# A delta-rule and attention kernel: the activation table is asked for ahead of each logarithm and exponential of the norms, not once per loop

## The chip, the cores and the metric

The kernel runs on one core of a Trainium2 chip. The metric is the device time of one execution in microseconds (us). The engines of the core have their own instruction streams and meet at semaphores: TensorE (PE, with its weight loads as PEld), VectorE (DVE), ScalarE (ACT), GpSimd (POOL) and SyncE (SP), which issues most of the DMAs. ScalarE evaluates functions such as exp, ln and tanh from a table set that is loaded into the engine by an instruction of its own, `ACT_TABLE_LOAD`.

## What is computed

512 tokens of width 1024 go through two blocks of the first kind (retention, forgetting attention, RWKV-7, a gated feed-forward part) and one of the second kind. The change touches only the second kind. Its mixer, cut to what matters:

```python
qkv_a, qkv_b, z_b, beta_b, alpha_b, gate_a, gate_b = split_columns(h @ w_in, IN_WIDTHS)
qa = rms_norm(qkv_a[:, :, 0], q_norm)            # local (dilated window) attention, 3 groups
ka = rms_norm(qkv_a[:, :, 1], k_norm)
...
qkv_b = causal_short_conv(qkv_b, conv_w)         # 4 taps, then SiLU
qb = l2_norm(qb.reshape(b, s, 8, 128)) * (128 ** -0.5)
kb = l2_norm(kb.reshape(b, s, 8, 128))
o_b = gated_delta_rule(qb, kb, vb, beta, g)      # chunked, 64 tokens each
o_b = rms_norm(o_b, dn_out_norm) * jax.nn.silu(z_b.reshape(b, s, 8, 128))
```

Each norm multiplies x by rsqrt(mean or sum of x*x, plus 1e-6) and a gain.

## The kernel before

Activations are kept transposed: 128 channels on the partitions, 512 tokens along the free axis, one tile of 128x512 per chunk of channels. The large projections are a stream ("flow") of units. A unit is one output tile: 8 columns of 128x128 weights, each multiplied three times (head by head, head by rest, rest by head, lines 370 to 372), since float32 weights and activations are split into a head and a rest. The weights of a piece (512 KB) are loaded by SP into one of four raw slots, ACT copies the head (`flow_head`, line 389) and DVE subtracts it for the rest (`flow_rest`, line 400).

All other stages are written into the same instruction streams. `flow.pe(t)`, `flow.act(t)` and `flow.dve(t)` put out everything of the flow that is due before tick t on their engine, at the place where they are called. What a unit leaves to ACT and DVE (evictions, convolution taps, the tanh of a gate) is a list of functions with due times, and it is put out in the same way. So the order on every engine is fixed when the program is built, and each engine works strictly in that order.

`unit_norm` (line 1921) is the norm of the window attention, of q and k of the delta rule, and of its output. It loops over n chunks (8 for q and k, 4 for the output). ACT squares a chunk (`square`, line 1950), PE sums the squares over the partitions (line 1935), ACT takes the logarithm out of the PSUM bank (line 1961) and then exp(-0.5 log) (`root`, line 1943), and DVE multiplies (line 1972). Squares are put out two chunks ahead of the logarithm. The names are `dn_sq`, `dn_rs` for q and k, `out_sq`, `out_rs` for the output and `win_sq`, `win_rs` for the windows. Between two chunks stands `flow.act`, with which the flow may put out a tanh there, of the convolution (`squash`, line 1826), or of the gates (line 1853).

`k.tables(name)` puts out a table load only where the set asked for is another than the one asked for last:

```python
def __call__(self, name):
    if name != self.held:
        self.nc.scalar.preload_act_table_set(name)
        self.held = name
```

`LN_EXP` names a set with ln and exp, `EXP_TANH` one with exp and tanh. Loads of this helper have line 420. Where a function stands in the program that the set at that place does not hold, a load is put ahead of it when the program is built, and it has the line of the function. The delta rule runs in two halves of four heads. In each, `unit_norm` for q and k is followed by `delta_pairs` (line 2368), whose PE part begins as follows and whose exponentials are `er` (line 2469) and `dl` (line 2471):

```python
pe.wait_ge(*k.gates_ready.at(2))
pe.wait_ge(*k.signals["un_log"].at(8))
```

Then follow the inversion of the triangular blocks, with four legs of small DMAs from ACT's queue (`blocks`, `spare_lanes`, `blocks_back`, `low_t`), the scan, and `unit_norm` for the output.

Of the kernel before, what the change touches and what calls it, by code (L numbers as in the profile page):

```python
# [41 lines left out]
LN_EXP = "natural_log_exp_and_others"  # L42
# [128 lines left out]
class Mark:  # L171
# [19 lines left out]
    def at(self, n):  # L191
        return self.sem, self.base + n
# [1728 lines left out]
def unit_norm(k, chunks, sums, scale, done, at, after=None):  # L1921


    nc, ps, flow, pe, v, a = k.nc, k.ps, k.flow, k.pe, k.v, k.a
    squared, summed, log, rstd = k.marks("un_squared", "un_sums", "un_log", "un_rstd")
    sq, rs, n = k.norm_sq, k.norm_rs, len(chunks)
    slots, roots = sq.shape[1], rs.shape[1]

    def tensor_part():
        for j in range(n):  # L1930
            flow.pe(at(j / n))
            pe.wait_ge(*squared.at(j + 1))
            if j >= 4:
                pe.wait_ge(*log.at(j - 3))
            nc.tensor.matmul(ps[j % 4][:, :], sums, sq[:, j % slots, :], start=True, stop=True).then_inc(*summed.up())  # L1935
        flow.pe(at(1))

    def scalar_part():
        k.tables(LN_EXP)

        def root(j):
            a.wait_ge(*log.at(j + 1))
            nc.scalar.activation(rs[:, j % roots, :], rs[:, j % roots, :], ACT.Exp, scale=-0.5).then_inc(*rstd.up())

        def square(j):
            if j >= slots:
                a.wait_ge(*summed.at(j - slots + 1))
            if chunks[j][3]:
                a.wait_ge(*chunks[j][3])
            nc.scalar.activation(sq[:, j % slots, :], chunks[j][0], ACT.Square).then_inc(*squared.up())  # L1950

        if after:
            a.wait_ge(*after)
        square(0)
        square(1)
        for j in range(n):
            flow.act(at(j / n))
            a.wait_ge(*summed.at(j + 1))
            if j >= roots:
                a.wait_ge(*done.at(done_base + j - roots + 1))  # L1960
            nc.scalar.activation(rs[:, j % roots, :], ps[j % 4][:, :], ACT.Ln, bias=k.const["eps6"], scale=scale).then_inc(*log.up())
            if j + 2 < n:
                square(j + 2)
            root(j)
        flow.act(at(1))

    def vector_part():
        for j in range(n):
            flow.dve(at((j + .5) / n))
            v.wait_ge(*rstd.at(j + 1))  # L1970
            src, gain, dst, _ = chunks[j]
            nc.vector.scalar_tensor_tensor(dst, src, gain, rs[:, j % roots, :], ALU.mult, ALU.mult).then_inc(*done.up())
        flow.dve(at(1))

    done_base = done.total - done.base
    tensor_part()
    scalar_part()
    vector_part()

# [1596 lines left out]
```

## Time and profile before

| | us |
|---|---|
| median of 3 runs | 3169.86 |
| lowest and highest of them | 3167.87, 3171.47 |
| span of the profiled execution | 3170.7 |
| PE busy in it | 2900.4 (91%) |
| DVE busy | 1704.2 (54%) |
| ACT busy | 1252.6 (40%) |
| table loads on ACT | 55 |

The span is the time from the first to the last instruction of one profiled execution. Starts are in us from its beginning. Busy shares are averages over stages with quite different limits, so the stages of the delta rule (about 2265 to 2630 us) are read one by one. The granted clock of TensorE is a share of full speed: 1.00 is 2.4 GHz and 0.50 is 1.2 GHz.

### The profile page before, as it was taken

The page shows a single profiled execution, that of the slowest core. Times are in us where ns is not written, and L with a number is a line of the kernel's source. Part 1 is how long each engine was busy: PE and PEld are TensorE (multiplying, and loading weights), DVE is VectorE, ACT ScalarE, POOL GpSimd, SP SyncE. Part 2 cuts the span into 40 slices and gives each one's busy share as a digit, 9 for nine tenths or more (in the row PEclk, how much of TensorE's full clock was granted, in tenths as well). Part 3 has the DMA queues.
Part 4 walks back from the last instruction along what each step waited for, and adds up shares of the span by engine and source line. Part 5 has one row for each costly group of instructions (what it writes and reads, how often), then busy time and mean ns, then how long its engine had stood idle before and what let it go on. Part 6 is the DMA issues. An engine that isn't in the chain of part 4 may idle for free.

```text
span 3170.7 us, 35407 instructions
## 1 busy us (share of the span) xinstructions
PE 2900.4 (91%) x13998; PEld 2291.2 (72%) x13998; DVE 1704.2 (54%) x2469; ACT 1252.6 (40%) x1913; POOL 14.8 (0%) x22
## 2 busy tenths in 40 slices
PE   6998899999999987999999999997688799969997
PEld 5566677888886666778888877775477677858885
DVE  3456535555334565355554335456574545459995
ACT  3233233333221342334332224454534434348873
POOL 0000000000000000000000000000000000000000
PEclk9999899999999999999999999998889899989998
DMA  4112113233331112022233321111110112359981
GB/s 162 47 40 63 44 41 93 97 96 100 92 124 62 44 51 63 28 89 88 98 99 114 99 94 54 60 60 47 33 47 28 45 36 87 98 216 370 396 323 53
DMA packets 96180, 307.70 MB, mean 97 GB/s; under 512 B 25744, under 2 KB 31760, under 8 KB 84240
## 3 DMA queue, kind: packets, MB, share of 16 engines
q1 hardware_dynamic: 69056, 284.88, 26.7%
q10 hardware_dynamic: 24368, 11.12, 1.2%
q0 software_dynamic: 2592, 9.44, 0.8%
q8 instruction: 112, 1.84, 0.2%
q14 instruction: 52, 0.43, 0.0%
HBM read 296.49 MB, written 8.91 MB: 96 GB/s over the span
## 4 chain that ended last, share of the span: by engine, by line
PE 77%; DVE 10%; ACT 6%; issue 4%; DMA 1%; ACTq 1%; POOL 0%; POOLq 0%; DVEq 0%
PE bank L370 19%; PE bank L372 18%; PE bank L371 18%; PE bank L365 2%; PE bank L367 2%; PE bank L366 2%; ACT flow_head L389 2%; DVE flow_rest L400 2%; PE bank L1935 1%; DVE dn L1818 1%; PE bank L2532 1%; PE bank L1238 1%; PE bank L1072 1%; PE bank L559 1%; PE bank L2017 0%
## 5 line engine op out<-in xcount | busy, mean ns | idle before, releaser
L400 DVE TENSOR_TENSOR flow_rest<-flow_raw,flow_head 128x1024 fp32r<-128x1024 f32 (+2 forms) x372 | 438.5, 1179 | 940.1 <-ACT flow_head L389 940.0
L370 PE MATMUL bank<-h_head,flow_head 128*128 128x512 f32 x2144 | 898.8, 419 | 34.2 <-DVE flow_rest L400 24.7
L371 PE MATMUL bank<-h_rest,flow_head 128*128 128x512 f32 x2144 | 846.7, 395 | 0.0
L372 PE MATMUL bank<-h_head,flow_rest 128*128 128x512 f32 x2144 | 846.3, 395 | 0.0
L389 ACT ACTIVATE flow_head<-flow_raw 128x1024 fp32r<-128x1024 f32 (+2 forms) x372 | 379.2, 1019 | 724.4 <-PE bank L372 677.2
L370 PEld LDWEIGHTS bank<-h_head,flow_head 128*128 128x128 f32 x2144 | 410.9, 192 | 155.1 <-issue 61.4
L371 PEld LDWEIGHTS bank<-h_rest,flow_head 128*128 128x128 f32 x2144 | 410.5, 191 | 92.0 <-issue 16.5
L372 PEld LDWEIGHTS bank<-h_head,flow_rest 128*128 128x128 f32 x2144 | 408.7, 191 | 89.0
L372 PE MATMUL bank<-ff_head,flow_rest 128*128 128x512 f32 x352 | 137.1, 389 | 0.0
L370 PE MATMUL bank<-ff_head,flow_head 128*128 128x512 f32 x352 | 137.1, 389 | 0.0
L371 PE MATMUL bank<-ff_rest,flow_head 128*128 128x512 f32 x352 | 137.1, 389 | 0.0
L400 DVE TENSOR_TENSOR flow_rest<-ring,flow_head 128x1024 fp32r<-128x1024 f32 x90 | 107.6, 1221 | 20.8 <-ACT flow_head L389 17.9
L400 DVE TENSOR_TENSOR late_rest<-ring,late_head 128x1024 fp32r<-128x1024 f32 x88 | 105.0, 1219 | 2.1 <-ACT late_head L389 0.4
L389 ACT ACTIVATE flow_head<-ring 128x1024 fp32r<-128x1024 f32 x90 | 94.7, 1061 | 22.0 <-PE bank L367 19.8
L389 ACT ACTIVATE late_head<-ring 128x1024 fp32r<-128x1024 f32 x88 | 93.3, 1062 | 18.9 <-PE bank L367 14.1
L370 PE MATMUL bank<-mh,flow_head 128*128 128x512 f32 x192 | 77.8, 405 | 5.9 <-DVE mr L1597 5.4
L1664 ACT ACTIVATE ff_head<-ff_up 128x512 fp32r<-128x512 f32 x44 | 27.8, 633 | 138.1 <-DVE ff_up L1660 138.1
L370 PE MATMUL bank<-yh,flow_head 128*128 128x512 f32 x96 | 43.8, 456 | 36.2 <-DVE sgf L1566 36.2
L371 PE MATMUL bank<-mr,flow_head 128*128 128x512 f32 x192 | 76.5, 398 | 0.0
L372 PE MATMUL bank<-mh,flow_rest 128*128 128x512 f32 x192 | 76.4, 398 | 0.0
L371 PEld LDWEIGHTS bank<-ff_rest,flow_head 128*128 128x128 f32 x352 | 66.1, 188 | 13.8
L372 PEld LDWEIGHTS bank<-ff_head,flow_rest 128*128 128x128 f32 x352 | 66.1, 188 | 13.7
(607 smaller groups left out, 4206.0 us busy)
## 6 DMA issues: line engine op xcount, KB each, us to landing
flow_raw<-in_w_in SPq DMA_DIRECT2D x176, 512.0 KB, 3.4
ring<-in_experts SPq DMA_DIRECT2D x84, 1024.0 KB, 7.3
flow_raw<-in_w_gate_up SPq DMA_DIRECT2D x88, 512.0 KB, 3.4
flow_raw<-in_w_down SPq DMA_DIRECT2D x32, 512.0 KB, 3.5
flow_raw<-in_w_out SPq DMA_DIRECT2D x24, 512.0 KB, 3.5
flow_raw<-in_paths SPq DMA_DIRECT2D x24, 256.0 KB, 2.6
flow_raw<-in_w_down SPq DMA_DIRECT2D x16, 384.0 KB, 3.1
flow_raw<-in_path_b SPq DMA_DIRECT2D x8, 512.0 KB, 3.4
```

The source lines that it names most:

```text
L365: nc.tensor.matmul(ps[bank][:, :], head, wh[:, c:c + S], start=start, stop=False)
L366: nc.tensor.matmul(ps[bank][:, :], head, wr[:, c:c + S], start=False, stop=False)
L367: last = nc.tensor.matmul(ps[bank][:, :], rest, wh[:, c:c + S], start=False, stop=stop)
L370: nc.tensor.matmul(ps[u.bank][:, :], wh[:, c:c + P], head, start=start, stop=False)
L371: nc.tensor.matmul(ps[u.bank][:, :], wh[:, c:c + P], rest, start=False, stop=False)
L372: last = nc.tensor.matmul(ps[u.bank][:, :], wr[:, c:c + P], head, start=False, stop=stop)
L389: nc.scalar.activation(self.parts_of[p.slot][0][:, 0:p.words], p.raw, ACT.Copy).then_inc(self.heads, 1)
L400: nc.vector.tensor_tensor(self.parts_of[p.slot][1][:, 0:p.words], p.raw, f32(self.parts_of[p.slot][0][:, 0:p.words]), ALU.subtract).then_i ...
L559: nc.tensor.matmul(ps[h // 2][b:b + HD, kt * P:S], v_tok[:, kt, h * HD:(h + 1) * HD], weighted[:, u % 4, 0:S - kt * P], start=kt == 0, sto ...
L1072: last = nc.tensor.matmul(ps[u % 4][:, q * 256:(q + 1) * 256], m[b:b + HD, jn, :], ar[b:b + HD, jn, :, :], start=True, stop=True)
L1238: last = nc.tensor.matmul(BX[c][:, m * P:m * P + n], CT[c][:, m, :], T[c][:, m, 0:n], start=True, stop=True)
L1818: ins = nc.vector.scalar_tensor_tensor(dst, k.pad[:, b, j:j + S], tap[:, j:j + 1], dst, ALU.mult, ALU.add)
```

## The change

`unit_norm` asks for the set `LN_EXP` in two more places: at the head of `root`, ahead of the exponential, and in the loop behind `flow.act`, ahead of the wait for the sum and the logarithm.

```diff
@@ -1939,6 +1939,7 @@
         k.tables(LN_EXP)
 
         def root(j):
+            k.tables(LN_EXP)
             a.wait_ge(*log.at(j + 1))
             nc.scalar.activation(rs[:, j % roots, :], rs[:, j % roots, :], ACT.Exp, scale=-0.5).then_inc(*rstd.up())
 
@@ -1955,6 +1956,7 @@
         square(1)
         for j in range(n):
             flow.act(at(j / n))
+            k.tables(LN_EXP)
             a.wait_ge(*summed.at(j + 1))
             if j >= roots:
                 a.wait_ge(*done.at(done_base + j - roots + 1))
```

Only ACT's stream differs; those of PE, DVE, SP and POOL hold the same instructions in the same order. ACT has 55 table loads before and 43 after, and every difference lies at three places.

ACT, norm of q and k of the first half, from the tanh of a convolution (line 1826) to the exponential of the fifth chunk; before:

```order
L1826 ACTIVATE sgf_179<-dn_0_185 128x512
L1961 ACT_TABLE_LOAD
L1961 ACTIVATE dn_rs<-bank,base_table 128x512
L1950 ACTIVATE dn_sq<-dn_1_183 128x512
L1943 ACT_TABLE_LOAD
L1943 ACTIVATE dn_rs<-dn_rs 128x512
L389 ACTIVATE flow_head<-flow_raw 128x1024
L1961 ACT_TABLE_LOAD
L1961 ACTIVATE dn_rs<-bank,base_table 128x512
L1950 ACTIVATE dn_sq<-dn_1_183 128x512
L1943 ACT_TABLE_LOAD
L1943 ACTIVATE dn_rs<-dn_rs 128x512
```

After, at the same place (logarithm, exponential and square now have lines 1963, 1944 and 1951):

```order
L1826 ACTIVATE sgf_179<-dn_0_185 128x512
L420 ACT_TABLE_LOAD
L1963 ACTIVATE dn_rs<-bank,base_table 128x512
L1951 ACTIVATE dn_sq<-dn_1_183 128x512
L1944 ACTIVATE dn_rs<-dn_rs 128x512
L389 ACTIVATE flow_head<-flow_raw 128x1024
L1963 ACTIVATE dn_rs<-bank,base_table 128x512
L1951 ACTIVATE dn_sq<-dn_1_183 128x512
L1944 ACTIVATE dn_rs<-dn_rs 128x512
```

One load stands behind the tanh where before each logarithm and each exponential up to the end of the loop had its own (ten in this norm).

ACT, end of the same norm and the first exponentials of `delta_pairs`; before:

```order
L1961 ACT_TABLE_LOAD
L1961 ACTIVATE dn_rs<-bank,base_table 128x512
L1943 ACT_TABLE_LOAD
L1943 ACTIVATE dn_rs<-dn_rs 128x512
L1826 ACTIVATE sgf_179<-dn_0_185 128x512
L2469 ACTIVATE er<-bank 128x512
```

After (`er` is line 2471 now):

```order
L1963 ACTIVATE dn_rs<-bank,base_table 128x512
L1944 ACTIVATE dn_rs<-dn_rs 128x512
L420 ACT_TABLE_LOAD
L1826 ACTIVATE sgf_179<-dn_0_185 128x512
L2471 ACTIVATE er<-bank 128x512
```

The tanh behind the loop has a load of its own now, since the set asked for last is `LN_EXP`.

ACT, norm of the first half's output and the beginning of the norm of q and k of the second half; before:

```order
L1826 ACTIVATE sgf_179<-dn_2_187 128x512
L1961 ACT_TABLE_LOAD
L1961 ACTIVATE out_rs<-bank,base_table 128x512
L1943 ACT_TABLE_LOAD
L1943 ACTIVATE out_rs<-out_rs 128x512
L389 ACTIVATE flow_head<-flow_raw 128x1024
L1961 ACT_TABLE_LOAD
L1961 ACTIVATE out_rs<-bank,base_table 128x512
L1943 ACT_TABLE_LOAD
L1943 ACTIVATE out_rs<-out_rs 128x512
L1853 ACTIVATE sgf_179<-sgf_179 128x512
L420 ACT_TABLE_LOAD
```

After:

```order
L1826 ACTIVATE sgf_179<-dn_2_187 128x512
L420 ACT_TABLE_LOAD
L1963 ACTIVATE out_rs<-bank,base_table 128x512
L1944 ACTIVATE out_rs<-out_rs 128x512
L389 ACTIVATE flow_head<-flow_raw 128x1024
L1963 ACTIVATE out_rs<-bank,base_table 128x512
L1944 ACTIVATE out_rs<-out_rs 128x512
L420 ACT_TABLE_LOAD
L1853 ACTIVATE sgf_179<-sgf_179 128x512
L420 ACT_TABLE_LOAD
```

Three loads are gone and one has come ahead of the tanh of line 1853. The third place, the last two chunks of the norm of q and k of the second half, has the same pattern: four loads of lines 1961 and 1943 become one, and one comes ahead of the next tanh of line 1853, behind three pairs of `er` and `dl`.

## Rows read from the trace of the kernel before

**Rows 1.** The page, part 1: busy time, share of the span, instructions.

```profile
PE 2900.4 (91%) x13998; PEld 2291.2 (72%) x13998; DVE 1704.2 (54%) x2469; ACT 1252.6 (40%) x1913; POOL 14.8 (0%) x22
```

**Rows 2.** Groups of ACT: count | busy us, mean ns | idle us before.

```profile
L420 ACT ACT_TABLE_LOAD x37 | 47.5, 1283 | 4.7 <-issue 4.1
...
L1961 ACT ACT_TABLE_LOAD x9 | 11.5, 1283 | 0.2
L1943 ACT ACT_TABLE_LOAD x9 | 11.5, 1283 | 0.2
```

**Rows 3.** Chain of waits, 2277.1 to 2300.1 us: shares of the stretch by line.

```profile
by line: ACT L1961 27.9%; issue 24.7%; ACT dn_rs L1961 15.0%; ACT L1943 11.5%; ACT dn_rs L1943 7.9%; ACT flow_head L389 4.5%; ACT dn L1813 3.1%; ACT sgf L1826 2.7%; ACT dn_sq L1950 2.7%; PE bank L2397 2.4%; ACT L420 2.0%; ACTq L1960 0.1%
```

**Rows 4.** Timeline of ACT, first half's norm: start, us, instruction, [idle before].

```profile
2280.96 0.62 ACT L1950 ACTIVATE dn_sq<-dn 128x512 f32<-128x512 f32 x1
2281.60 1.28 ACT L1943 ACT_TABLE_LOAD   x1
...
2282.89 0.63 ACT L1943 ACTIVATE dn_rs<-dn_rs 128x512 f32<-128x512 f32 x1
...
2283.43 1.04 ACT L389 ACTIVATE flow_head<-flow_raw 128x1024 fp32r<-128x1024 f32 x1
...
2293.37 0.63 ACT L1943 ACTIVATE dn_rs<-dn_rs 128x512 f32<-128x512 f32 x1
...
2295.32 0.69 ACT L1961 ACTIVATE dn_rs<-bank,base_table 128x512 f32<-128x512 f32 x1
...
2299.26 0.69 ACT L1961 ACTIVATE dn_rs<-bank,base_table 128x512 f32<-128x512 f32 x1
```

**Rows 5.** Timeline of ACT where no load stands between the functions.

```profile
2274.37 0.62 ACT L1950 ACTIVATE dn_sq<-dn 128x512 f32<-128x512 f32 x1
2274.89 0.62 ACT L1943 ACTIVATE dn_rs<-dn_rs 128x512 f32<-128x512 f32 x1
2275.41 0.68 ACT L1961 ACTIVATE dn_rs<-bank,base_table 128x512 f32<-128x512 f32 x1
...
2622.35 0.69 ACT L1961 ACTIVATE out_rs<-bank,base_table 128x512 f32<-128x512 f32 x1 [0.46 <-PE bank L1935]
2623.07 0.63 ACT L1943 ACTIVATE out_rs<-out_rs 128x512 f32<-128x512 f32 x1
```

**Rows 6.** Timeline of PE, first half's norm and the start of `delta_pairs`.

```profile
2287.04 2.08 PE L1935 MATMUL bank<-dn_sq,base_table 128*128 128x512 f32 x2 [3.58 <-ACT dn_sq L1950]
...
2292.11 1.13 PE L1935 MATMUL bank<-dn_sq,base_table 128*128 128x512 f32 x2 [1.09 <-ACT dn_sq L1950]
...
2300.09 2.05 PE L2397 MATMUL bank<-table_2b,g 128*128 128x128 f32 x8 [6.16 <-ACT dn_rs L1961]
```

**Rows 7.** Timeline of DVE, the same stretch.

```profile
2284.50 1.22 DVE L400 TENSOR_TENSOR flow_rest<-flow_raw,flow_head 128x1024 fp32r<-128x1024 f32 x1 [4.71 <-ACT flow_head L389]
2285.64 0.74 DVE L1972 SCALAR_TENSOR_TENSOR dn<-dn,base_table,dn_rs 128x512 f32<-128x512 f32 x1
...
2286.31 0.68 DVE L1809 TENSOR_TENSOR pad<-bank,root 128x512 f32<-128x512 f32 x1
...
2294.71 2.32 DVE L1818 SCALAR_TENSOR_TENSOR dn<-pad,pk,dn 128x512 f32<-128x512 f32 x3
...
2303.98 0.69 DVE L2440 TENSOR_TENSOR kb<-dn,bank 128x512 f32<-128x512 f32 x1 [1.31 <-PE bank L2403]
```

**Rows 8.** By stretch: us, busy of ACT, granted clock, DMA share, GB/s.

```profile
2300.09:2303.50 3.41, 2.79 (x4) 0.50 0.00 0
```

**Rows 9.** Timeline of PE: first sum and first `delta_pairs` product, second half.

```profile
2461.42 2.08 PE L1935 MATMUL bank<-dn_sq,base_table 128*128 128x512 f32 x2 [9.88 <-ACT dn_sq L1950]
...
2484.94 2.05 PE L2397 MATMUL bank<-table_2b,g 128*128 128x128 f32 x8 [5.68 <-ACT dn_rs L1961]
```

**Rows 10.** Timeline of PE: a sum of a window norm behind a shorter wait.

```profile
2105.78 2.08 PE L1935 MATMUL bank<-win_sq,table_2b 128*128 128x512 f32 x2 [2.67 <-ACT win_sq L1950]
```

**Rows 11.** DMA issues, 2330 to 2372 us: KB each, median us to landing.

```profile
flow_raw<-in_w_in SPq DMA_DIRECT2D x4, 512.0 KB, 3.5
blocks<-low_t ACTq DMA_DIRECT2D x8, 16.0 KB, 1.7
```

## The prediction

> **What bounds the kernel now.** I read the page first. PE is busy for 91% of the span and ACT for 40% [rows 1], which says only that ACT is no bound on the average. What counts is whether ACT is the bound where the loads stand. The groups of ACT show 55 table loads of 1.283 us each, 37 asked for by the kernel and 18 put ahead of a logarithm or an exponential of `unit_norm` (nine and nine) [rows 2]. The idle time ahead of these 18 is 0.2 us in each group, so ACT goes straight from the function before into the load.
>
> The chain of waits over 2277.1 to 2300.1 us is almost nothing but ACT: loads of lines 1961, 1943 and 420, then the functions they serve [rows 3]. PE waits there: 3.58 us, 1.09 us and then 6.16 us for ACT [rows 6]. The same picture stands in the second half: PE waits 9.88 us for the first square of the second norm and 5.68 us for its last logarithm [rows 9]. At all three places ACT sets the end, and DVE and PE behind it can only start later or earlier by what ACT does.
>
> **What the change does.** Only ACT's stream changes. Of the 18 loads all go; three come back behind the tanh inside the loops, and three come ahead of the tanh that follows each place. The net is 12 loads, 12 x 1.283 = 15.4 us of ACT's busy time.
>
> **Price of a load on the path.** From a square to the exponential behind it is 2282.89 - 2280.96 = 1.93 us with a load between [rows 4] and 2274.89 - 2274.37 = 0.52 us without [rows 5]. So a load costs 1.41 us: its own 1.28, and about 0.1 us by which two neighbours would have overlapped. From an exponential to a logarithm it is 2295.32 - 2293.37 = 1.95 us [rows 4] against 0.52 us [rows 5], a price of 1.43. From a logarithm to its own exponential there is no overlap to win (0.72 us without a load, 2623.07 - 2622.35 [rows 5]); there it is the load alone, 1.28.
>
> The Trainium skill, "ScalarE: Activation LUTs", section "What ACT_TABLE_LOAD costs", gives some 1.28 us for the load and 1.38 us for a drain, about 2.66 us for each switch. The load agrees with this trace; the drain does not, since the load here begins 0.02 us after the end of the square, at 2281.60, and the exponential begins 0.01 us after the load. By the page's total the three places would give about twice my sum, an estimate of some 30 us.
>
> **First place, norm of q and k, first half.** The load at 2279.08 stays under another line. Up to the last logarithm at 2299.26, which releases PE's first product of `delta_pairs` at 2300.09, eight loads go: seven at 1.41 to 1.43 and one, between a logarithm and its exponential, at 1.28. That is 11.1 us.
>
> Not all of it comes, as one cover is gone. The last tap of the convolution (line 1813, on ACT) needs `pad` from DVE, and before it came late enough. Now the exponential is at 2280.96 + 0.52 = 2281.48 and `flow_head` at 2282.0. DVE follows by the distances of [rows 4, 7]: `flow_rest` 1.07 us later (2283.07), the multiply 1.14 later (2284.21), `pad` 0.67 later (2284.88), done at 2285.6. ACT would be free for the tap at 2284.6 (logarithm 2283.0, square 2283.6, exponential 2284.1). It waits about 1.0 us. The last logarithm comes at about 2289.1 and PE starts `delta_pairs` 0.83 us behind it, as now (2300.09 - 2299.26), at 2289.9: 10.2 us earlier.
>
> There is a second part on PE. After its wait of 6.16 us the granted clock is 0.50, the lower level of 1.2 GHz, for the 3.41 us to 2303.5 [rows 6, 8], while it did not fall behind the wait of 1.09 us (two sums in 1.13 us against 2.08 us) [rows 6]. Squares now come early, so that by the same walk PE's waits in this norm are 0.9 us at most; I take the clock to stay at 2.4 GHz. Then the products of lines 2397 and 2403 take 1.9 us instead of 3.8 and end at 2291.8. The next step, `kb` on DVE, needs these and the last multiply. DVE, in its order, does the sixth multiply at 2288.0, the three taps (2.32 us [rows 7]), the seventh multiply at 2290.9 and the eighth at 2291.6, and so reaches `kb` at 2292.3, against 2303.98 [rows 7]: 11.7 us earlier. DVE's multiplies hide the rest of PE's gain. If the clock falls after all, it is 10.2.
>
> The load that comes ahead of the tanh of line 1826 has `er` queued behind it, and DVE's next step after `kb` waits for `er`. Last exponential 2289.8, load 2290.5 to 2291.8, tanh 2291.8, `er` 2292.3 to 2292.9, and DVE wants it at 2292.9. It is covered by the multiplies and by `kb`, without a margin; with that cover gone it costs up to 1.3 us. I take 0.1. First place: **11.6 us**, between 8.9 and 11.7.
>
> **Second place, norm of the output, first half.** Three loads go ahead of the tanh of line 1853 (1.28 between logarithm and exponential, 1.41 behind `flow_head`, 1.28 again) and one comes ahead of it (1.41 back). The next load, ahead of the squares of the second norm, stays. PE waits for just these squares. Net 4.0 - 1.4 = **2.5 us**, rounded down for small gaps. The tanh needs a DVE step that by the same distances is ready at the time the added load ends, so nothing new waits, and the wait of 9.88 us stays above 7: PE's clock is at 1.2 GHz behind it as before.
>
> **Third place, last two chunks of the second norm.** Two loads stand ahead of the last logarithm that PE waits for: 1.28 + 1.43 = **2.7 us**. The third is ahead of the last exponential, off the path. The added load comes ahead of a tanh in the middle of `delta_pairs`, where PE is full and ACT waits for DVE; I cost it at nothing, 0.2 us without that cover. PE's wait falls from 5.68 to 3.0 us [rows 9]. The row nearest to that is a wait of 2.67 us with the same 2.08 us for two sums behind it [rows 10], so the clock falls here still. If not, 1.7 us more.
>
> **Sum.** 11.6 + 2.5 + 2.7 = 16.8 us; the ends are 8.9 + 2.5 + 2.7 = 14.1 and 11.7 + 2.6 + 4.4 = 18.7. What follows is carried by semaphores from these points, and the chain of waits runs through them, so it shifts as a whole. Against the profiled span it gives 3170.7 - 16.8 = 3153.9. That span is 0.8 us above the median of the runs, and I take the gain off the median: 3169.9 - 16.8 = **3153.1 us**.
>
> **Rivals.**
> - PE's clock holds at the third place too: 18.5 us, 3151.4 us. For it: the wait is shorter than any before `delta_pairs` now. Against it: [rows 10]. Chance 0.08.
> - What comes next swallows the first place: the stage behind it has another pace-maker, the stream of weights from SP, which doesn't come earlier. Then only 5.2 us stay, 3164.7 us. Against it: SP loads a piece as soon as `flow_head` and `flow_rest` have freed a slot, these come earlier too, a piece lands in 3.5 us [rows 11], and PE and DVE wait for no DMA in these rows. Chance 0.06.
> - Slower: the inversion in each half has four legs of small DMAs that ACT issues and waits for, and SP's 512 KB loads share the DMA engines. The legs are now shifted against the loads. A leg that lands in 1.7 us now could stand behind a load of 3.5 us [rows 11]. If all eight legs did, they would cost 28 us and the kernel would be 11 us slower, 3181 us. It decides from five legs on (17.5 us); the loads are triggered by the same engines and shift along, which speaks against it. Chance 0.02.
> - A switch of tables costs ACT more than its row shows, so that 30 us go: 3140 us. The distances in [rows 4, 5] exclude it nearly. Chance 0.02. It is the result by the page's total above.
> - That the change does not do what it says is out: after it ACT's stream holds 43 loads.
>
> **How the numbers follow.** The forecast has 0.82. Its bounds give 3151 to 3156 us, and the three runs of before lie 3.6 us apart. The range 3148 to 3160 takes in this spread and the first rival. A run of this kernel can tell about 0.2%, 6.3 us, from no change: faster means below 3163.5 us. Forecast, first and fourth rival are faster (0.92), the second is within 0.2% (0.06), the third is slower (0.02).
>
> **What would show it.** In the profile of the changed kernel ACT has 43 loads, all under line 420. In the first norm PE's waits for squares are below 1.2 us, the first product of `delta_pairs` begins near 2290 at full clock, and `kb` near 2292. PE's wait for the second norm's first square is some 7.4 us and the second `delta_pairs` begins 16.8 us earlier than 2484.94, near 2468, behind a wait of 3 us and at the lower clock. I am wrong if the tap's wait for `pad` is much longer than 1 us, if `er` holds DVE up, or if the interval from there to the end is longer than before.

## The result and the profile after

| | before | after |
|---|---|---|
| median of the runs with the first result, us | 3170.7 | 3154.0 |
| ratio, 95% interval | | 0.9943 (0.9929 to 0.9957) |
| span of the profiled execution, us | 3170.7 | 3151.4 |
| table loads on ACT | 55 | 43 |

The changed kernel is 16.7 us faster by these medians, 13.6 to 22.5 us by the interval. One of its four runs was slow (4186.2 us, mean granted clock 0.648), and the ratio goes by the other three, whose median is 3153.2 us. It was measured twice more beside the experiments below, with ratios of 0.9934 (0.992 to 0.9948) and 0.9944 (0.993 to 0.9957). Over all three measurements the median of its 13 runs compared is 3152.2 us, against 3170.6 us of the 32 runs of the kernel before that stand beside them and the experiments: 18.5 us. The forecast was 3153.1 us.

The page and the groups of ACT after, to be read beside [rows 1, 2]:

```profile
PE 2895.7 (92%) x13998; PEld 2286.2 (73%) x13998; DVE 1704.1 (54%) x2469; ACT 1236.9 (39%) x1901; POOL 14.8 (0%) x22
```

```profile
L420 ACT ACT_TABLE_LOAD x43 | 55.2, 1283 | 4.9 <-issue 4.1
```

ACT lost 12 instructions and 15.7 us of busy time. DVE, with the same instructions, kept its own. PE shows 4.7 us less, but a second profile of the kernel before has 2897.9 us and two more of the changed kernel 2893.0 and 2896.9, so the size of that is not shown.

ACT in the first half's norm of q and k after (start, us, instruction, idle before), the place of [rows 4]:

```profile
2274.97 0.63 ACT L1826 ACTIVATE sgf<-dn 128x512 f32<-128x512 f32 x1
2275.61 1.28 ACT L420 ACT_TABLE_LOAD   x1
2276.91 0.69 ACT L1963 ACTIVATE dn_rs<-bank,base_table 128x512 f32<-128x512 f32 x1
2277.49 0.62 ACT L1951 ACTIVATE dn_sq<-dn 128x512 f32<-128x512 f32 x1
2278.01 0.62 ACT L1944 ACTIVATE dn_rs<-dn_rs 128x512 f32<-128x512 f32 x1
2278.53 1.04 ACT L389 ACTIVATE flow_head<-flow_raw 128x1024 fp32r<-128x1024 f32 x1
...
2282.13 0.72 ACT L1813 ACTIVATE dn<-pad,pk 128x512 f32<-128x512 f32 x1 [0.94 <-DVE pad L1809]
...
2285.61 0.67 ACT L1963 ACTIVATE dn_rs<-bank,base_table 128x512 f32<-128x512 f32 x1
2286.32 0.63 ACT L1944 ACTIVATE dn_rs<-dn_rs 128x512 f32<-128x512 f32 x1
...
2286.97 1.28 ACT L420 ACT_TABLE_LOAD   x1
...
2288.26 0.63 ACT L1826 ACTIVATE sgf<-dn 128x512 f32<-128x512 f32 x1
2288.80 0.58 ACT L2471 ACTIVATE er<-bank 128x512 f32<-128x512 f32 x1
```

One load stands behind the tanh, none is inside the loop, and one comes behind it. The square and the exponential behind it are 0.52 us apart. The tap waits 0.94 us for `pad`. PE and DVE at the same place, beside [rows 6, 7]:

```profile
2280.72 1.12 PE L1935 MATMUL bank<-dn_sq,base_table 128*128 128x512 f32 x2 [0.73 <-ACT dn_sq L1951]
...
2284.00 1.13 PE L1935 MATMUL bank<-dn_sq,base_table 128*128 128x512 f32 x2 [0.76 <-ACT dn_sq L1951]
...
2286.43 1.13 PE L2399 MATMUL bank<-table_2b,g 128*128 128x128 f32 x8 [0.61 <-ACT dn_rs L1963]
...
2287.39 1.06 PE L2405 MATMUL bank<-base_table,mbeta 128*128 128x128 f32 x8
2287.41 1.41 DVE L1974 SCALAR_TENSOR_TENSOR dn<-dn,base_table,dn_rs 128x512 f32<-128x512 f32 x2
...
2288.85 0.69 DVE L2442 TENSOR_TENSOR kb<-dn,bank 128x512 f32<-128x512 f32 x1
```

PE's waits fell from 3.58, 1.09 and 6.16 us to 0.8 us and less, and its first eight products of `delta_pairs` take 1.13 us instead of 2.05. `kb` follows DVE's last two multiplies without a wait. The chain of waits from the load ahead of the tanh to `kb` (2273.6 to 2288.9 us, shares by line) can be read beside [rows 3], where no line of DVE stands. Now DVE has over half of it:

```profile
by line: DVE dn L1974 22.4%; DVE dn L1818 14.3%; ACT dn_rs L1944 11.5%; ACT L420 11.4%; issue 11.1%; ACT dn_rs L1963 8.8%; DVE flow_rest L400 8.0%; ACT flow_head L389 6.2%; DVE kb L2442 4.5%; ACT sgf L1826 4.1%; DVE pad L1809 3.9%; ACT dn_s
```

PE in the second half, beside [rows 9], and the granted clock behind its second wait (us, busy of PE, PEld, DVE, ACT and POOL, clock, DMA share, GB/s):

```profile
2445.06 2.08 PE L1935 MATMUL bank<-dn_sq,base_table 128*128 128x512 f32 x2 [7.29 <-ACT dn_sq L1951]
...
2465.53 1.13 PE L2399 MATMUL bank<-table_2b,g 128*128 128x128 f32 x8 [2.99 <-ACT dn_rs L1963]
```

```profile
2465.50:2467.60 2.10, 2.07 (x17) 2.08 (x18) 1.44 (x3) 1.14 (x2) 0.00 (x0) 1.00 0.00 0
```

The waits are the ones forecast, 7.3 and 3.0 us. Behind the second the clock stayed at 1.00, 2.4 GHz, where I had taken it to fall.

**Where the time went.** Starts in two executions differ by some us even where nothing is changed, so I compare stretches between instructions that both kernels have. "Norm 1" is from the first square of the first half's norm to `kb`; "output" from the table load ahead of the output norm to the first square of the second half's norm; "norm 2" from there to `kb` of the second half. The table has every profile of the two kernels.

| us | before | before, second profile (e11) | after | after (e8) | after (e10) |
|---|---|---|---|---|---|
| first square at | 2267.3 | 2266.3 | 2263.8 | 2260.9 | 2266.5 |
| norm 1 | 36.68 | 36.69 | 25.08 | 25.04 | 25.04 |
| `kb` to output norm | 137.04 | 137.06 | 138.37 | 138.31 | 138.32 |
| output | 19.72 | 19.72 | 17.16 | 17.16 | 17.17 |
| norm 2 | 27.86 | 27.85 | 23.31 | 23.32 | 23.32 |
| sum of these four | 221.30 | 221.32 | 203.92 | 203.83 | 203.85 |
| second `kb` to the end | 682.1 | 679.7 | 683.7 | 682.6 | 680.1 |

The three changed stretches give 11.6 + 2.56 + 4.5 = 18.7 us and repeat to a few hundredths of a microsecond. The stretch from `kb` to the output norm, in which no load was taken out, gives 1.3 us back in all three profiles of the changed kernel. From the first square to the second `kb` it is 17.4 us shorter. The first row and the last one vary by 6 and 4 us, with no relation to the kernel that shows.

The 1.3 us stand in two waits of DVE for PE, in the inversion of the first half, the first two lines from before and the next two from after:

```profile
2367.83 0.69 DVE L2557 TENSOR_TENSOR inv_ct<-low_t,level_t 128x512 f32<-128x512 f32 x1 [1.67 <-PE bank L2532]
2392.98 0.69 DVE L2557 TENSOR_TENSOR inv_ct<-low_t,level_t 128x512 f32<-128x512 f32 x1 [1.77 <-PE bank L2532]
...
2353.34 0.69 DVE L2559 TENSOR_TENSOR inv_ct<-low_t,level_t 128x512 f32<-128x512 f32 x1 [2.37 <-PE bank L2534]
2379.18 0.69 DVE L2559 TENSOR_TENSOR inv_ct<-low_t,level_t 128x512 f32<-128x512 f32 x1 [2.48 <-PE bank L2534]
```

PE, ahead of the second of them, comes out of the same wait in both kernels, and the granted clock behind it differs (before, then after; the last two lines are stretches as above):

```profile
2387.22 0.66 PE L2519 MATMUL bank<-base_table,inv_tt 128*128 128x128 f32 x4 [3.04 <-DVE inv_tt L2567]
...
2372.72 2.32 PE L2521 MATMUL bank<-base_table,inv_tt 128*128 128x128 f32 x8 [3.03 <-DVE inv_tt L2569]
```

```profile
2387.20:2389.00 1.80, 1.23 (x9) 0.99 (x10) 1.80 (x4) 0.72 (x2) 0.00 (x0) 1.00 0.73 273
...
2372.70:2375.00 2.30, 2.19 (x9) 1.79 (x10) 2.30 (x4) 0.72 (x2) 0.00 (x0) 0.50 0.59 205
```

Before, the clock fell only behind the first products; after, it had fallen already. Around the first of DVE's two waits the clock is 1.00 before (2365.2 to 2368.0 us) and 0.80 after (2350.3 to 2353.4 us).

### The profile page after: what moved, and what is told of

Same layout as the page of the kernel before. It is cut to its first block, busy times and chain, and to the rows that moved or that the text cites. A ratio compares the mean times of both kernels' runs of the same rounds, so it can differ in the third digit from the quotient of the medians.

```text
span 3151.4 us, 35395 instructions
## 1 busy us (share of the span) xinstructions
PE 2895.7 (92%) x13998; PEld 2286.2 (73%) x13998; DVE 1704.1 (54%) x2469; ACT 1236.9 (39%) x1901; POOL 14.8 (0%) x22
## 4 chain that ended last, share of the span: by engine, by line
PE 77%; DVE 10%; ACT 6%; issue 4%; DMA 2%; ACTq 1%; POOL 0%; POOLq 0%; DVEq 0%
PE bank L370 19%; PE bank L372 18%; PE bank L371 18%; PE bank L365 2%; PE bank L367 2%; PE bank L366 2%; ACT flow_head L389 2%; DVE flow_rest L400 2%; PE bank L1935 1%; DVE dn L1818 1%; DMA h_rows<-tokens 1%; PE bank L2534 1%; PE bank L1238 1%; PE bank L1072 1%; ACT L420 1%
## 5 line engine op out<-in xcount | busy, mean ns | idle before, releaser
L370 PE MATMUL bank<-ff_head,flow_head 128*128 128x512 f32 x352 | 136.9, 389 | 0.0
L371 PE MATMUL bank<-ff_rest,flow_head 128*128 128x512 f32 x352 | 136.9, 389 | 0.0
L372 PE MATMUL bank<-ff_head,flow_rest 128*128 128x512 f32 x352 | 136.9, 389 | 0.0
L400 DVE TENSOR_TENSOR flow_rest<-ring,flow_head 128x1024 fp32r<-128x1024 f32 x90 | 107.7, 1221 | 20.8 <-ACT flow_head L389 17.7
L372 PEld LDWEIGHTS bank<-ff_head,flow_rest 128*128 128x128 f32 x352 | 66.1, 188 | 13.8
L371 PEld LDWEIGHTS bank<-ff_rest,flow_head 128*128 128x128 f32 x352 | 66.1, 188 | 13.8
L370 PEld LDWEIGHTS bank<-ff_head,flow_head 128*128 128x128 f32 x352 | 66.1, 188 | 13.5
```

The source lines that it names most:

```text
L370: nc.tensor.matmul(ps[u.bank][:, :], wh[:, c:c + P], head, start=start, stop=False)
L371: nc.tensor.matmul(ps[u.bank][:, :], wh[:, c:c + P], rest, start=False, stop=False)
L372: last = nc.tensor.matmul(ps[u.bank][:, :], wr[:, c:c + P], head, start=False, stop=stop)
L400: nc.vector.tensor_tensor(self.parts_of[p.slot][1][:, 0:p.words], p.raw, f32(self.parts_of[p.slot][0][:, 0:p.words]), ALU.subtract).then_i ...
```

## The experiments

The theory to be tested, A: each load at these places lies on the path, costs what its row shows, and its removal is carried to the end. Rivals: B, a good part of the difference is of the execution (the changed kernel's profile was 3.5 us ahead before the first changed place); C, a switch costs 2.66 us. For one place at a time I use shorter intervals, named in the expectations. In the two kernels they are 25.54 and 13.88 us (first), 19.72 and 17.16 (second), 11.67 and 7.47 (third).

**e1_first**: the request in the loop for one norm alone.

```diff
             flow.act(at(j / n))
+            if k.norm_sq is k.dn_sq and not after:
+                k.tables(LN_EXP)
             a.wait_ge(*summed.at(j + 1))
```

> The request in the loop is made only in the first half's norm of q and k; the other two places keep their loads. Intervals are read from the trace. First: start of the tanh of line 1826 inside the norm to start of kb, 25.5 us before and 13.9 us after. Second: table load ahead of the output norm's first square to the first square of the next norm, 19.7 before and 17.2 after. Third: table load ahead of the tanh inside the second half's norm to kb, 11.7 before and 7.5 after. Theory A (every load there lies on the path and the gain is carried to the end): first interval 13.9, second 19.7, third 11.7, time 11 to 12 us below before. Theory B (a good part of the difference of 16.7 us is of the execution, as the changed kernel was 3.5 us ahead before the first place was reached): the first interval is the same, but the time falls by 8 us or less.

Measured: 13.89, 19.72 and 11.90 us; the median is 3161.0 against 3172.1 us of the runs beside it, 11.1 us less, ratio 0.9963 (0.995 to 0.9976). From the first square to the second `kb` it is 209.68 us, 11.6 less than before, and the medians show as much at the end. The interval of the runs, 7.6 to 15.9 us, only just reaches the 8 us that B allows; e11_before below and the two later measurements of the changed kernel take B's ground away.

**e2_second** and **e3_third**: the same with the conditions below.

```diff
+            if k.norm_sq is k.out_sq:
+                k.tables(LN_EXP)
```

> The request is made only in the norm of the output. Theory A: first interval 25.5, second 17.2, third 11.7 us. If the loads of the second place were hidden by PE's or DVE's work the second interval would stay at 19.7.

```diff
+            if k.norm_sq is k.dn_sq and after:
+                k.tables(LN_EXP)
```

> The request is made only in the second half's norm of q and k. Theory A: first 25.5, second 19.7, third 7.5 us, of which 2.7 is two loads and 1.5 is PE's clock, which holds since PE waits 3.0 us. If the clock falls the third interval is 9.0.

Measured: e2_second 25.54, 17.16 and 11.90 us, 3168.9 us in its one run, where 2.6 us less than before can't be told. e3_third 25.54, 19.72 and 8.55 us, 3165.3 us. The second place was on the path as forecast. The third gave 3.1 us of its interval here and 4.2 in the changed kernel, against 11.67 us; the difference is PE's clock. PE in e3_third, and the clock of the stretch:

```profile
2475.38 1.40 PE L2399 MATMUL bank<-table_2b,g 128*128 128x128 f32 x8 [2.98 <-ACT dn_rs L1963]
2476.57 1.92 PE L2405 MATMUL bank<-base_table,mbeta 128*128 128x128 f32 x8
```

```profile
2475.30:2478.50 3.20, 3.12 (x17) 3.15 (x18) 1.49 (x3) 1.19 (x2) 0.00 (x0) 0.62 0.00 0
```

The wait is the same, 2.98 us against 2.99, and the clock still fell, within the first eight products. A wait of 3.0 us at this place is followed by either.

e2_second also bears on the row "`kb` to output norm" of the table: it has the program of before in that stretch, and 138.20 us, not 137.05. e3_third, with that program too, has 136.9, and e4_root, where the first place is changed, 137.0. But the three profiles of the changed kernel, e1_first and e5_wait all have 138.3 to 138.4, and both of before 137.0. So the 1.3 us are not in the program of the stretch; they come with PE's clock, and the changed kernel paid them in every profile of it. Whether it must is not shown.

The clock moves the second norm as well. From its first square to the load ahead of its tanh ACT has one program in all runs up to e6_loads, and took 16.2 us before, 15.8 in the changed kernel, but 14.6, 15.2 and 14.6 in e1 to e3. e1_first, with all loads of the third place kept, has 26.54 us in norm 2 instead of 27.86. So the 4.5 us of norm 2 in the table are not the price of its loads alone.

**e4_root**: only the request ahead of the exponential.

```diff
         def root(j):
+            k.tables(LN_EXP)
             a.wait_ge(*log.at(j + 1))
```

> Only the request ahead of the exponential is made, not the one ahead of the logarithm. Then a logarithm behind a tanh has its own load, and its exponential another: one load more at each of the three places than in the changed kernel (46 loads). Theory A: first interval 13.9 + 1.4 = 15.3, second 17.2 + 1.3 = 18.5, third 7.5 + 1.3 = 8.8 if PE's clock holds behind a wait of 4.3 us and 10.3 if it falls; time 12 to 13 us below before. Theory C (a switch costs 2.66 us): first 16.5, second 19.8, third 10.1 or more.

Measured: 15.31, 18.45 and 10.38 us, so one load more at each place costs 1.43, 1.29 and, with the clock falling behind a wait of 4.26 us, 2.91 us. The first two are A's 1.4 and 1.3; C's 2.66 is out. The median is 3154.4 us, 17.7 us below before, ratio 0.9949 (0.9933 to 0.9966): more than the 12 to 13 us forecast for it from the first result. From the first square to the second `kb` it is 207.50 us, 13.8 less than before. By the three intervals it should lie 5.6 us above the changed kernel; the runs can't tell that closely. ACT at the first place in e4_root:

```profile
2277.35 1.28 ACT L1962 ACT_TABLE_LOAD   x1
2278.64 0.69 ACT L1962 ACTIVATE dn_rs<-bank,base_table 128x512 f32<-128x512 f32 x1
2279.23 0.62 ACT L1951 ACTIVATE dn_sq<-dn 128x512 f32<-128x512 f32 x1
2279.86 1.28 ACT L420 ACT_TABLE_LOAD   x1
2281.16 0.63 ACT L1944 ACTIVATE dn_rs<-dn_rs 128x512 f32<-128x512 f32 x1
```

The load of line 1962 is the one put ahead of a logarithm, that of line 420 the one asked for, and behind the second no more follow until the next tanh. e1 to e3 do without the request in `root` and have the changed kernel's intervals, apart from what the clock adds in e3, so it is the request ahead of the logarithm that does the work. The one in `root` never finds another set, since nothing of the flow stands between the two.

**e5_wait**: the changed kernel with a redundant load ahead of the logarithm that PE waits for.

```diff
             k.tables(LN_EXP)
+            if k.norm_sq is k.dn_sq and after and j == 7:
+                nc.scalar.preload_act_table_set(LN_EXP)
             a.wait_ge(*summed.at(j + 1))
```

> The changed kernel with one more table load, ahead of the last logarithm of the second half's norm of q and k, so that PE waits 4.3 us instead of 3.0 us for its first product of delta_pairs. Its set is the one that is loaded already. If PE's clock holds: third interval 7.5 + 1.4 = 8.9 us. If it falls, as behind the waits of 3.6 us and more of the kernel before: 10.4 us, and line 2399's eight products take 2.05 us instead of 1.13.

Measured: 10.03 us, 2.6 more than the changed kernel's 7.47.

```profile
2465.33 1.46 PE L2401 MATMUL bank<-table_2b,g 128*128 128x128 f32 x8 [4.41 <-ACT dn_rs L1965]
2466.58 1.91 PE L2407 MATMUL bank<-base_table,mbeta 128*128 128x128 f32 x8
```

The clock fell, as in e4_root, though a little later than the expectation had it (1.46 us for the first eight products, not 2.05). Of the 2.6 us 1.4 are the load (the wait grew from 2.99 to 4.41 us) and the rest is the clock. A load of the set that is held already costs as much as a switch.

**e6_loads**: seven more loads at the first place (of eight asked for, one beside another load was not put out).

```diff
             k.tables(LN_EXP)
+            if k.norm_sq is k.dn_sq and not after:
+                nc.scalar.preload_act_table_set(LN_EXP)
             a.wait_ge(*summed.at(j + 1))
```

> The changed kernel with a table load more ahead of each of the 8 logarithms of the first half's norm of q and k. Walked through by the distances of the trace: the first two are hidden by ACT's waits for the sums (1.7 and 2.0 us), one behind a load costs 1.28, the one ahead of the fifth logarithm 0.5 as the wait for pad takes 0.9 of it, four cost 1.4 each. Theory A: the last logarithm comes 7.4 us later; the time is 7 to 9 us above the changed kernel (the 2 for PE's clock, which falls if its waits pass 2.7 us). Theory C (2.66 us a load): 14 us or more.

Measured: from the first square to the last logarithm 27.87 us against 21.84 in the changed kernel, 6.0 more. With the missing load's 1.28 taken off the 7.4 of the walk, 6.1 were due (the first two loads stand in ACT's waits for the sums and cost nothing). The tap no longer waited for `pad`: the loads took that cover, as forecast. The median is 3158.6 us, ratio 0.9963 (0.9949 to 0.9976), 6.5 us above the pooled changed kernel and 9.5 above the one measured beside it, where 7 to 9 were forecast. C, 14 or more for eight loads, would have been 11 or more for these seven. That the clock falls once a wait passes 2.7 us, as the expectation has it, does not hold: it stayed up behind the third place's 2.98 us in this same run. At the first place PE waited 3.44 us and then had its first products at full clock, the next ones at the lower:

```profile
2295.62 1.13 PE L2401 MATMUL bank<-table_2b,g 128*128 128x128 f32 x8 [3.44 <-ACT dn_rs L1965]
2296.58 1.87 PE L2407 MATMUL bank<-base_table,mbeta 128*128 128x128 f32 x8
```

**e7_late**: what is left is a tanh and two loads inside each of the three norms. The due times of these three tanhs are put later, so that they come behind the loops (ticks of the flow's units; 12 and 23 are the convolution units in question).

```diff
             seen = hf * 12 + n
+            late = {12: 7.5, 23: 3.5}.get(seen, 0)
...
-                                 [(1, keep), (3, taps), (8, silu)], [(2, last_tap), (6, squash)]))
+                                 [(1, keep), (3, taps), (8 + (late if seen == 12 else 0), silu)], [(2, last_tap), (6 + late, squash)]))
...
-            flow.unit(6 + q if b == 0 else 4 + q, [(pieces[q], c * P) for c in range(DC)], operand(False), [(1, scale)], [(2, squash)])
+            flow.unit(6 + q if b == 0 else 4 + q, [(pieces[q], c * P) for c in range(DC)], operand(False), [(1, scale)],
+                      [(4.5 if (b, i0, q) == (0, 0, 1) else 2, squash)])
```

> The changed kernel with the three tanhs that fall into the norms (two of the convolution, one of a gate) given later due times, so that they come behind the loops. No load stands inside a loop any more: 36 to 37 loads. Theory A: up to the last logarithm or the next norm's first square each place is 2.7 to 3.4 us shorter; at the first and third place er comes 0.5 to 1.2 us later behind the loop. Sum 5 to 8 us below the changed kernel, about 3147 us. Rival: PE or the wait for pad is the bound once the loads are gone, and it stays within 2 us of the changed kernel.

Measured: 3146.2 us, ratio 0.9926 (0.9912 to 0.9939), 2.9 us below the changed kernel beside it, less than the 5 to 8 us forecast. From the first square to the second `kb` it is 5.7 us shorter than in that kernel (198.2 against 203.8), so the time is near the forecast 3147 us, but the gain is not clear in the runs. Norm 1 22.27 us instead of 25.04 and norm 2 19.95 instead of 23.32, but the output stretch 18.26 instead of 17.16. DVE and ACT there:

```profile
2439.58 0.63 ACT L1827 ACTIVATE sgf<-dn 128x512 f32<-128x512 f32 x1
2440.24 0.69 DVE L1831 SCALAR_TENSOR_TENSOR dn<-sgf,dn 128x512 f32<-128x512 f32 x1 [5.29 <-ACT sgf L1827]
2440.85 1.22 DVE L400 TENSOR_TENSOR flow_rest<-flow_raw,flow_head 128x1024 fp32r<-128x1024 f32 x1
...
2442.65 0.68 DVE L1849 TENSOR_TENSOR sgf<-bank,root 128x512 f32<-128x512 f32 x1
...
2443.37 0.63 ACT L1854 ACTIVATE sgf<-sgf 128x512 f32<-128x512 f32 x1 [3.16 <-DVE sgf L1849]
```

The tanh came later but DVE's step that uses it (line 1831) kept its place, so DVE stood 5.29 us with everything behind it, among that the step for which ACT's next tanh waits.

**e9_late2** leaves the convolution's tanh in the output norm where it was (`late = {12: 7.5}`); **e10_after** is the changed kernel beside it, **e8_after** that beside e7_late.

> As e7_late, but only the tanhs inside the two norms of q and k are put out later; the one inside the output norm keeps its due time, since in e7_late DVE stood 5.3 us behind it and the next gate's tanh then waited 3.2 us for DVE. Theory A: second interval 17.2 us again instead of 18.3, first norm's first square to kb 22.3 and second norm's first square to kb about 20.0 us as in e7_late; sum 2.8 + 3.3 = 6 us less in these stretches than in the changed kernel. Rival: what follows gives it back (er comes 1 us later behind the loop), and it stays within 2 us of the changed kernel.

> The changed kernel a third time, for comparison with e9_late2 on the same chip. Intervals 13.9 and 17.2 us, and 7.5 us where PE's clock holds behind its wait of 3.0 us, up to 8.6 where it falls during the first products as in e3_third. Time 16 to 21 us below before.

> The changed kernel again, to have it on the same chip as the others: 16 to 17 us below before. Theory B: the part of it that lies before the first place (3.5 us in the first profile) differs in this execution, while the three intervals stay 13.9, 17.2 and 7.5 us.

Measured: e9_late2 3147.6 us, ratio 0.9923 (0.9909 to 0.9936); e10_after 3152.2 us, 0.9944; e8_after 3149.2 us, 0.9934, which is 20.8 us below before where 16 to 17 were expected. The stretches of e9_late2 are 22.27, 17.16 and 20.53 us (22.3, 17.2 and about 20.0 expected), against 25.04, 17.17 and 23.32: 5.6 us less, of which 4.5 us show in the medians. e7_late and e9_late2 can't be told apart by their runs (3146.2 and 3147.6 us, 23.7 and 24.0 us below the runs beside them). All five runs of e9_late2 lie below the five of e10_after, but the intervals of the ratios overlap a little, so that it beats the changed kernel is shown by the trace and only likely by the runs. The rival, that what follows gives it back, does not hold for most of it: DVE waits 0.40 us for `er` behind the first loop, and from the first square to the second `kb` the kernel is 6.2 us shorter than e10_after.

**e11_before**: the kernel before a second time.

> The kernel before, profiled a second time, to see what of the difference upstream of the first place is of the execution. Theory B: the first square of the first norm starts anywhere between 2260 and 2268 us, as in the other profiles, whose program is the same up to there; the intervals stay 25.5, 19.7 and 11.7 to 11.9 us.

Measured: first square at 2266.3 us, intervals 25.54, 19.72 and 11.66 us (11.90 in e1 and e2). Over all profiles, with one program up to that square, it comes between 2260.9 and 2267.3 us. So the 3.5 us by which the first profile of after was ahead were the execution's.

## Why the prediction was right, point by point

- **What bounds the kernel.** Right at all three places; e1, e2 and e3 removed the loads of one place each, and each interval shrank with its own place alone.
- **Price of a load, 1.41 to 1.43 and 1.28 us.** Right. e4 gave 1.43 and 1.29, e6 6.0 us for seven loads where 6.1 were due by these prices. The figure of 2.66 us a switch from the Trainium skill, "ScalarE: Activation LUTs", section "What ACT_TABLE_LOAD costs", is not what a switch costs here; its 1.28 us for the load itself is.
- **First place, 11.6 us.** Right, 11.6. (Its eight loads add up to 11.2 us by its own prices, where it says 11.1; the profiles give 10.1 for the last logarithm plus 0.94 for the tap's wait.) So were its parts: the tap's wait, 1.0 forecast and 0.94 found; PE's waits, 0.9 at most and 0.8 found; the clock, which stayed at 2.4 GHz; `kb` bound by DVE's multiplies; and the load ahead of `er`, hidden with next to no margin (`er` ends at 2289.4, DVE's next step starts at 2289.5).
- **Second place, 2.5 us.** 2.56.
- **Third place, 2.7 us.** Here a term was mis-sized: it gave 4.2 in its interval and 4.5 us from the norm's first square. The two loads gave their 2.7. The step that failed is "the clock falls here still", taken from the nearest row, a wait of 2.67 us in front of a window norm [rows 10]. In all three profiles of the changed kernel it did not fall behind 2.99 us, which gave 1.5 us; the remaining 0.3 lies ahead of the tanh in the same norm, where unchanged programs differ by more. I had this as the first rival, at 0.08 and 1.7 us; with it the sum is 18.5, and the three stretches measure 18.7. One row was too thin for a choice between two levels, and it was not the nearest: the same trace has a wait of 3.04 us at 2387.2 us behind which the first products ran at full clock (shown above). The two together would have called the choice open.
- **That all is carried to the end, and what follows "shifts as a whole".** Right for what the loads gave, by e1. But the stretch behind the first place was taken to keep its length, and it grew by 1.3 us through PE's clock, a term that the sum has at nothing. The traces give 17.4 us from the first square to the second `kb`, the forecast was 16.8, and the pooled medians give 18.5; which of the two measured numbers is nearer can't be told, since the rest of the program varies by 4 us. That the forecast came so near is luck in part: the clock gave 1.5 us more than forecast at the third place and took 1.3 us in between.
- **The rivals.** That the weights' stream swallows the gain: no, by e1. Slower through the DMA legs: the stretch with the first half's legs was 1.3 us longer in the changed kernel, but in two waits for PE at the lower clock, while a leg (`blocks`) landed in 1.7 us at the median in both kernels. Dearer switches: no, by e4 and e6.

## What to carry to other kernels

A helper that skips a table load when the set asked for last is the same must be called ahead of every function that needs a certain set, at least wherever other work can be put out between: if it is called once ahead of a loop and a function of another set comes into the loop, the build mends each function by itself, and each logarithm and each exponential then gets a load of its own until the loop ends. To price a load, take the distance of its neighbours with and without it at the same two functions (here 1.3 to 1.4 us), and then look for what the loads had hidden, here a wait of 0.9 us for DVE. When moving a function later on one engine, move its user on the next engine too, or that engine stands still with all that is queued behind it.

## What the runs showed of the hardware

- PE's clock behind a wait is not decided by the wait alone. At the third place it stayed at 2.4 GHz behind 2.98 to 2.99 us in four profiles (the three of the changed kernel and e6_loads) and fell during the first eight products in e3_third with a wait of 2.98 us. In the inversion, behind 3.04 us, it held through the first products before and was already at 1.2 GHz in the changed kernel (3.03 us). Behind 2.67 us of a window norm it was at 1.2 GHz at once before [rows 10], where the same two sums took 1.64 us in the changed kernel instead of 2.08. Behind 3.44 us (e6_loads) the first eight products had full clock and the next eight not. Behind the first-place and third-place waits of 4.26, 4.41, 5.7 and 6.2 us it fell every time. With the lower level behind the wait the third interval was some 1.5 us longer. What decides between 2.7 and 3.5 us I did not settle.
- A load of the table set that is held already took the same time as a switch (e5, e6).
- Executions of one program reached the same instruction, some 2260 us in, at times that lay 6 us apart, while the three changed stretches, 17 to 37 us long, repeated to 0.05 us from profile to profile of one kernel. An effect of 2 us was found by the stretches, never by the medians. Such a stretch still holds what the clock did in it, so between two kernels it shifted by up to 1.5 us with its own program unchanged.
